# Issuing layer two's expert weights from SyncE and ScalarE in turn, with another order of work in the routing

## What is computed

```python
def _ec_moe(h, router, w_gate, w_up, w_down):
    B, n, _ = h.shape
    cap = CAPACITY_FACTOR * n // N_EXPERTS
    aff = jax.nn.softmax((h @ router).astype(jnp.float32), axis=-1)
    g, idx = lax.top_k(jnp.swapaxes(aff, 1, 2), cap)
    bidx = jnp.arange(B)[:, None, None]
    xs = h[bidx, idx]
    a = jnp.einsum('becd,edf->becf', xs, w_gate)
    u = jnp.einsum('becd,edf->becf', xs, w_up)
    y = jnp.einsum('becf,efd->becd', jax.nn.silu(a) * u, w_down) * g[..., None].astype(h.dtype)
    return jnp.zeros_like(h).at[bidx, idx].add(y)
```

## Time and profile before

| | us |
|---|---|
| median of 3 runs | 1863.23 |
| lowest and highest | 1861.32, 1863.63 |
| the profiled execution | 1864.48 |
| its span in the profile | 1862.6 |
| TensorE busy | 1764.9 (95%) |
| VectorE busy | 798.4 (43%) |
| ScalarE busy | 357.3 (19%) |
| GpSimd busy | 229.8 (12%) |

### The profile page before, as it was taken

The page is one execution under the profiler, slowest core; times in us unless marked ns, Lnnn a source line. Parts: engine busy times, 40 slices in busy tenths (PEclk is TensorE's granted clock), DMA queues, the critical chain, the costliest instruction groups (busy, mean ns, idle before and its releaser), DMA issues.

```text
span 1862.6 us, 30900 instructions
## 1 busy us (share of the span) xinstructions
PE 1764.9 (95%) x13222; PEld 900.6 (48%) x13222; DVE 798.4 (43%) x1624; ACT 357.3 (19%) x776; POOL 229.8 (12%) x313
## 2 busy tenths in 40 slices
PE   7999999999899999999999999999989999888896
PEld 4886567744344444444443886577433333222222
DVE  3994767678511111111112674776242333223232
ACT  3313455622100000000001313555210000000001
POOL 1000331011111112121111001410010000000000
PEclk9999999999899999999999999999999999999999
DMA  9644000086799999999997843001869999999996
GB/s 397 233 151 161 1 1 2 1 343 261 266 396 400 392 394 393 392 402 394 395 393 288 341 158 135 1 24 47 340 253 401 402 403 404 412 407 408 412 412 273
DMA packets 83137, 525.68 MB, mean 282 GB/s; under 512 B 11280, under 2 KB 13600, under 8 KB 24128
## 3 DMA queue, kind: packets, MB, share of 16 engines
q1 hardware_dynamic: 66672, 478.66, 63.9%
q0 software_dynamic: 14128, 44.84, 7.8%
q10 hardware_dynamic: 2208, 0.26, 0.1%
HBM read 506.94 MB, written 16.79 MB: 281 GB/s over the span
## 4 chain that ended last, share of the span: by engine, by line
PE 75%; DMA 15%; DVE 5%; ACT 3%; issue 1%; SPq 0%; POOL 0%; POOLq 0%; DVEq 0%; ACTq 0%
PE psum L1621 16%; PE psum L1615 9%; PE psum L1624 8%; DMA arena<-in_w_up 8%; PE psum L1495 7%; PE psum L1305 6%; PE psum L1263 6%; DMA ring<-in_w_up 6%; PE psum L1381 5%; PE psum L1426 3%; PE psum L1399 2%; PE psum L1355 2%; ACT arena L1086 2%; PE psum L1701 2%; PE psum L1339 2%
## 5 line engine op out<-in xcount | busy, mean ns | idle before, releaser
L1621 PE MATMUL psum<-ring,arena 128*32 128x512 f32 x1856 | 242.1, 593 | 0.0
L1615 PE MATMUL psum<-ring,arena 128*64 128x512 f32 x888 | 206.4, 600 | 19.4 <-DMA ring<-in_w_down 12.3
L1172 ACT ACTIVATE arena<-psum 128x768 f32<-128x768 f32 (+1 forms) x32 | 22.5, 704 | 894.5 <-PE psum L1624 463.3
L1615 PE MATMUL psum<-arena 128*64 128x512 f32 x648 | 151.3, 600 | 13.4 <-DMA arena<-in_w_up 7.4
L1495 PE MATMUL psum<-ring,arena 128*128 128x512 f32 x320 | 143.1, 598 | 0.8 <-DVE arena L2008 0.8
L1624 PE MATMUL psum<-ring,arena 128*32 128x256 f32 x1856 | 142.7, 379 | 0.0
L1086 ACT ACTIVATE arena<-psum,smx 128x768 f32<-128x768 f32 (+4 forms) x160 | 118.9, 748 | 96.4 <-DVE smx L1979 96.4
L1615 PEld LDWEIGHTS psum<-ring,arena 128*64 128x64 f32 x888 | 58.3, 136 | 151.1 <-issue 109.5
L1979 DVE TENSOR_REDUCE smx<-psum 128x1 f32<-128x768 f32 (+4 forms) x160 | 115.8, 765 | 30.9 <-PE psum L1339 23.9
L1624 PEld LDWEIGHTS psum<-ring,arena 128*32 128x32 f32 x1856 | 60.3, 110 | 138.8 <-issue 138.8
L1621 PE MATMUL psum<-arena 128*32 128x512 f32 x960 | 125.2, 593 | 0.0
(11 more groups left out here) (318 smaller groups left out, 2069.3 us busy)
## 6 DMA issues: line engine op xcount, KB each, us to landing
ring<-in_w_down SPq DMA_DIRECT2D x85, 1024.0 KB, 28.3
ring<-in_w_up SPq DMA_DIRECT2D x80, 1024.0 KB, 28.2
ring<-in_w_gate SPq DMA_DIRECT2D x78, 1024.0 KB, 28.0
arena<-in_w_gate SPq DMA_DIRECT2D x50, 1024.0 KB, 29.0
arena<-in_w_up SPq DMA_DIRECT2D x48, 1024.0 KB, 27.3
arena<-in_w_down SPq DMA_DIRECT2D x43, 1024.0 KB, 28.0
ring<-in_w_adat SPq DMA_DIRECT2D x32, 1024.0 KB, 6.3
ring<-in_w_in SPq DMA_DIRECT2D x18, 1024.0 KB, 19.9
```

Source lines behind the costliest of these rows:

```text
L1615: ins = mm(psum[64 * n:64 * n + 64, b * 512:(b + 1) * 512], lhs(k), w[:, n * 512:(n + 1) * 512], start=k == 0, stop=k == KD - 1)
L1621: ins = mm(psum[r0:r0 + 32, b * 512:(b + 1) * 512], lhs(k)[:, 32 * g:32 * g + 32], w[:, n * 512:(n + 1) * 512], start=k == 0, stop=k == KD ...
```

## The change

Four things change.

1. Expert weights of layer two: from m = 21 on SyncE issues the even quarters and ScalarE the odd ones (86 of them). SyncE skips those. ScalarE's program takes silu(0) first; then it goes through its quarters, waits for each one's place, issues it, and takes silu(e) as soon as the next place to wait for is one that comes free after the gate of e.
2. Layer one's quarters: 11 waits for the latent gather (`gl`); 12 to 14 wait only for w_out; 15 waits for expert 1's gather (`gat` at 32), the turned rows and the stores.
3. The routing's order. TensorE: in block 4's turn the logits of block 3 come after w_out's group 3 instead of 5, and the lists are turned there; the lists come across before the last group of block 5; the filler of three goes to one; the last logit parts come after the turn of the gathered latents. VectorE: affinities, lists, choosing, output and merging of the latents all lie in t = 4; the copy of turned rows goes ahead of the reciprocal in the last block; unit u = 2t + 1 of the ahead sums is made at t instead of t + 1, and GpSimd loads units 2t + 2 and 2t + 3 at t. ScalarE: the load of the exponential table goes behind the last copies, in both layers.
4. Attention: narrow steps alternate between half banks, so that the scores of a narrow step behind another wait for the exponentials of two steps before.

```diff
+    def narrow(st):
+        return st.kind == "W" and len(st.blocks) == NC
     def scores_at(st, x):
-        return 1024 * x
+        return 1024 * x + (512 * (st.i % 2) if narrow(st) else 0)
...
+    def by_scalar(l, m):
+        return l == DEPTH - 1 and m >= TURN[l] and m % 2 == 1
...
                     m = m0 + q
+                    if by_scalar(l, m):
+                        continue
...
+                    if l < DEPTH - 1 and m == RING + EARLY[l] - 1:
+                        sp.wait_ge(*LS[l]("gl", 16))
                     if m == RING + EARLY[l]:
                         sp.wait_ge(free, spent(where[("wout", l)]) + 4)
+                    if m == RING + EARLY[l] + UNDER_HT:
                         if l < DEPTH - 1:
-                            sp.wait_ge(*LS[l]("gl", 16))
+                            sp.wait_ge(*LS[l]("gat", 32))
                             sp.wait_ge(*LS[l]("ot", nq(l)))
...
-                    for u in (2 * t + 1, 2 * t + 2):
+                    for u in (2 * t + 2, 2 * t + 3):
...
-                if t == nq(l) - 1:
-                    act.activation(rootx[:], eps[:], ACT.Exp)
...
                 act.activation(lgpart[t % 2], bank(7, P, P * (t % 2)), ACT.Copy).then_inc(L["lc"], 1)
+                if t == nq(l) - 1:
+                    act.activation(rootx[:], eps[:], ACT.Exp)
...
+                silu(0, unit_no(l, 0, UP))
+                e = 1
+                for m, which, expert, q in long_units(l):
+                    if not by_scalar(l, m):
+                        continue
+                    place_free = spent(where[("exp", l)]) + m + 1 - TURN[l]
+                    if e < NE and place_free >= unit_no(l, e, GATE + 4 - UNITS_E):
+                        silu(e, unit_no(l, e, GATE + 4 - UNITS_E))
+                        e += 1
+                    dst, sem_of, _ = long_place(l, m)
+                    act.wait_ge(free, place_free)
+                    act.dma_start(dst.rearrange("p (k n) -> p k n", k=2), wv[which][expert, q]).then_inc(sem_of, 16)
+                while e < NE:
+                    silu(e, unit_no(l, e, GATE + 4 - UNITS_E))
+                    e += 1
...
+                if st.i >= 2 and apart(st):
+                    pe.wait_ge(*L("exp", 2 * st.i - 2))
+                elif st.i:
                     pe.wait_ge(*L("exp", 2 * st.i))
...
-                    slots_across(0)
-                    kept_busy(4, 3)
+                    kept_busy(4, 1)
...
-                if i == NX + 1:
-                    turn_lists(0)
+                sooner = i == NX and not last
                 if i < nq(l):
-                    mixed_rows(i, range(2, 4))
-                if i >= 1:
+                    mixed_rows(i, range(2, 3 if sooner else 4))
+                if i >= 1 and i != NX + 2:
                     logit_parts(i - 1)
+                if sooner:
+                    mixed_rows(i, range(3, 4))
+                    logits(i - 1)
                 if i < nq(l):
                     mixed_rows(i, range(4, 6))
+                if sooner:
+                    turn_lists(0)
...
                     ins.then_inc(L["xtl"], 1)
-                if i >= 1:
+                    logit_parts(i - 1)
+                if i >= 1 and not sooner:
                     logits(i - 1)
                 if i < nq(l):
-                    mixed_rows(i, range(6, 8))
+                    mixed_rows(i, range(6, 7))
+                if i == NX + 1:
+                    slots_across(0)
+                if i < nq(l):
+                    mixed_rows(i, range(7, 8))
...
                 if t == NX:
                     shifted(0)
+                    affinities(0)
+                    lists_in(0)
+                    for r in range(0, 2):
+                        best_eight(0, r)
...
-                if t == NX + 1:
-                    latents_merged()
                 tt(row_x(l, t), row_x(l, t), part, ALU.add).then_inc(L["x1"], 1)
                 if t == NX:
-                    affinities(0)
+                    best_eight(0, 2)
...
                 if not last and t < NX:
-                    if t >= 1:
-                        ahead_sums(2 * t - 1)
                     ahead_sums(2 * t)
+                    if t < NX - 1:
+                        ahead_sums(2 * t + 1)
                 if t == NX:
-                    lists_in(0)
-                    for r in range(CAPX // 8):
+                    for r in range(3, CAPX // 8):
                         best_eight(0, r)
                     slots_out(0)
+                    latents_merged()
```

More of the change, by code:

```diff
@@ L182, in build_program @@
     EARLY = [0, 4]
+    UNDER_HT = 3
+    assert UNDER_HT * SLOT == 8 * T
     assert DEPTH == 2
@@ L652, in expert_loads, with long_units @@
         return ([(0, 0)] if e == 0 else []) + [(1, e)] + ([(0, e + 1)] if e < NE - 1 else []) + [(2, e)]
+    def by_scalar(l, m):
+        return l == DEPTH - 1 and m >= TURN[l] and m % 2 == 1
+    def long_units(l):
+        m = 0
+        for e in range(NE):
+            for which, expert in expert_loads(l, e):
+                for q in range(4):
+                    yield m, which, expert, q
+                    m += 1
     def unit_no(l, e, m):
@@ L1172, in silu @@
                 act.activation(sg[l][:, 0:n_col], psum[:, 1024:1024 + n_col], ACT.Silu).then_inc(L["silu"], 1)
[L1174 to L1177, removed]
+            if l < DEPTH - 1:
+                for e, _ in body_experts(act):
+                    silu(e, unit_no(l, e, UP) if isinstance(e, int) and e == 0
+                         else unit_no(l, e, GATE + 4 - UNITS_E))
+                silu(NE - 1, unit_no(l, NE - 1, GATE + 4 - UNITS_E))
+            else:
+                silu(0, unit_no(l, 0, UP))
+                e = 1
+                wv = [w[l] for w in (w_gate, w_up, w_down)]
+                for m, which, expert, q in long_units(l):
[11 more added lines that the diff above has]
+                    e += 1
             act.activation(rootx[:], eps[:], ACT.Sqrt)
@@ L1327, in _, with apart @@
             steps = ATT[l]
+            def apart(st):
+                return narrow(st) and narrow(steps[st.i - 1])
             def scores(st):
-                if st.i:
+                if st.i >= 2 and apart(st):
+                    pe.wait_ge(*L("exp", 2 * st.i - 2))
+                elif st.i:
                     pe.wait_ge(*L("exp", 2 * st.i))
@@ L2092, in shifted @@
                 dve.wait_ge(*L("lg", b1))
+                dve.wait_ge(*L("orc", b1))
                 for t in range(b0, b1):
@@ L2182, in _ @@
                 dlink(dve, tt(part, bank(2 * (t % 2), D), g1row[s], ALU.mult))
-                if t == NX + 1:
-                    latents_merged()
                 tt(row_x(l, t), row_x(l, t), part, ALU.add).then_inc(L["x1"], 1)
                 if t == NX:
-                    affinities(0)
-                dve.wait_ge(*L("ort", t + 1))
-                dve.reciprocal(stat[:, 2, t:t + 1], stat[:, 1, t:t + 1]).then_inc(L["orc"], 1)
+                    best_eight(0, 2)
+                if t < nq(l) - 1:
+                    dve.wait_ge(*L("ort", t + 1))
+                    dve.reciprocal(stat[:, 2, t:t + 1], stat[:, 1, t:t + 1]).then_inc(L["orc"], 1)
                 dve.wait_ge(*L("ot", t + 1))
```

## The result

The changed kernel takes 1872.15 us (median), the kernel before, in runs beside it, 1863.63: a ratio of 1.0045, interval 1.0034 to 1.0056. It is slower by 8.5 us, and outside the range of 1857.5 to 1869. In the profiled executions the span grew by 7.7 us, from 1862.6 to 1870.3.

| start of | before | after | shift | change since the row above | forecast |
|---|---|---|---|---|---|
| w_out, layer one | 376.80 | 375.29 | -1.5 | -1.5 | -0.5 |
| turn of expert 1's rows | 508.71 | 496.89 | -11.8 | -10.3 | -6.9 + 0.6 |
| layer two's projections | 1023.79 | 1020.80 | -3.0 | +8.8 | +0.9 |
| w_out, layer two | 1293.66 | 1291.27 | -2.4 | +0.6 | 0 |
| first product of layer two's experts | 1386.28 | 1383.56 | -2.7 | -0.3 | -0.9 |

What follows compares the result with a forecast made beforehand. Layer one was taken as led by TensorE with DMA also full, layer two as set by weight landings. Terms -6.0 + 0.6 - 0.5 - 0.9 + 0 + 2.3 + 4.9 = +0.4 gave 1863.6 us, range 1857.5 to 1869.

Steps and rivals of the forecast that it cites:

- The end of layer two: Last weight landings of layer two: two queues with equal turns keep SyncE's head start, quarter 187 lands later, +4.9 us.
- The start: Layer two's first expert quarters: ScalarE issues quarter 21 only behind silu(0), the DMA engines lose time, +2.3 us (0.5 to 3).
- The issue: ScalarE's issues in layer two's experts: 2.1 us each in front of its silus, absorbed before UP's quarters land, nothing.
- The rate: Weights' transfer rate in layer two on two queues: packet for packet in turn and no faster, 0 (-5.6 to +2).
- Routing in layer one: Between layer one's attention and first joint product: earlier scaling and faster gathers, less the stream's cost, -6.0 us (-2.5 to -7.5).
- What that costs: Layer one's held quarters: TensorE's lead of 7.3 us becomes 7.3 - 6.9 - 1.2 = -0.8, so it waits some 0.9 us.
- the sign that the forecast had named for its fall: End of layer one: the forecast falls if that layer ends less than 4 us sooner.
- the attention: Narrow steps of layer one's attention may start their scores one step sooner, -0.5 us (-1.8 to 0).
- the ahead units: Unit 3 of the ahead sums, loaded and summed one block sooner, holds up VectorE's add of t=1, +0.6 us (0 to 3).
- Layer two's routing: The exponential table's load moves behind the last copy of turned rows, off the last logits' path, -0.9 us (-1.5 to 0).
- Rival 2: Layer one: gathers stay slow alone, held quarters make the stream 4.8 us late, routing gives 2.5; 1867.1 us, chance 0.16.
- Rivals 1, 3 and 4: 1: odd quarters keep up, 1859.1 us, 0.17; 3: two queues faster, 1858.0, 0.09; 4: second queue changes nothing, 1856.4, 0.08.

## Why the prediction was wrong

**The end of layer two** was right: +4.9 forecast, +5.0 measured. The head start of SyncE's queue is made in the first microseconds and kept for 450, as the equal packet counts of the earlier trace rows said; the run with the last 24 quarters on SyncE gave back 4.9, and the one with ScalarE first showed that the head start comes from the issue behind silu(0).

**The start** was right: +2.3 forecast, 2.4 measured. ScalarE's first quarter went out 0.6 us sooner than forecast, with silu(0) issued and not yet done.

**The issue** was right in what it came to, nothing, and not in its size: ScalarE's issues took 3.3 and 3.6 us in the rows above, not 2.1, and SyncE's 0.33. Five of the fifteen later silus came behind such an issue, and TensorE waited for none of them.

**The rate** was wrong: 0 was taken, with +2 as the upper end; it cost 2.9 us in 410. The step put "packet for packet in turn and no faster: 0" between two windows of the earlier trace rows with no gather in either. The windows were right, the rate away from gathers is 421 GB/s on one queue and on two, but the stage has a gather per expert, and with these beside it the second queue is not free: 405 GB/s instead of 408. The row that would have told was that of the whole stage in the earlier trace rows: 409 GB/s against the 423 of a stretch without a gather. That gap of 14 GB/s was there to be explained; without gathers it is gone, and with the second queue it is larger. The Trainium skill (DMA: Bandwidth & Descriptors, "Issuing engines are not separate DMA queues") says that issuing from several engines saves the issue time alone. The pair without gathers agrees, 421 and 421; with gathers 3 us were lost.

**Routing in layer one** failed at the step "What that costs", and there at the sum 7.3 - 6.9 - 1.2 = -0.8. The mechanism was the right one, but its main size and one of its ends were off. Counted from w_out's start, the gain was 10.3 us and not 6.9. The scaling came 4.4 us sooner, as forecast, but none of it was lost on the way: the latents were turned 4.9 us sooner and not 3.75. GATE0 followed this by 2.9 us and not by 3.45 + 0.4, and so began 5.4 us sooner and not 3.3. From there to the turn of expert 1's rows 4.9 us fell away and not 3.56: the waits shrank by 2.4 only, but TensorE's work took 2.5 us less at a granted clock of 1.00 instead of 0.89. The clock stood in no term of the sum. The stream of weights then ended 0.3 us later from w_out on, and not 1.2. Against a TensorE that is 10.3 us sooner the lead of 7.3 was overdrawn by 3.3: the sum reads 7.3 - 10.3 - 0.3 = -3.3 instead of -0.8. What I left out is the end: when TensorE is that far ahead of the stream, the residual rows' loads run beside the last quarter and the weights behind it, and VectorE waits for these too. TensorE ended layer one's products 6.5 us sooner and began the next layer 3.0 us sooner. Of 11.8 us, 8.8 went back, where the forecast had 0.9. So the sign that the forecast had named for its fall, layer one ending less than 4 us sooner, came. The thirteen traces show what a better step would have said: the next layer's first expert product follows the landing of layer one's last quarter by 378.4 to 381.0 us, so here the new order was worth what it did to the stream and little more.

**The rest**: the attention gave 1.5 us with all that precedes it (0.5 forecast; runs differ by that much there, so it is not shown), the ahead units cost nothing to be seen, where +0.6 was forecast. Layer two's routing gained 0.3 instead of 0.9: its lists and its gather were some 1.4 us sooner within the stage, and the filler at a lower clock gave 1.1 of it back.

**Of the rivals**, none came. Rival 2 had the right place, layer one's stream and the held quarters, but the wrong cause: the gathers were as fast as hoped, and the loss came anyway. Two of its figures were wrong besides: the context gather had five quarters beside it before and not six, and with the gathers' 2.46 and 1.97 us added to 500.7 its landing is 505.1 and not 504.3, which makes its time 1868.0 us and not 1867.1. Rivals 1, 3 and 4 fell with the order of the landings and with the rate.

In sum: -6.0 + 0.6 for layer one's routing became -1.5 (3.9 us more), 0 for the rate became 3, and smaller terms (-1.0 up to w_out, +0.6 in layer two's projections and attention, +0.6 in its routing) make up the rest of the way from +0.4 to +7.7 in the span.

## What to carry to other kernels

Where two resources are both nearly full, as TensorE and the DMA engines were in layer one, a stage that starts sooner need not end sooner (11.8 us became 3.0): find the last landing and ask what the change does to that. An ordered stream split over two queues kept the head start that one of them got at the first issue to the end, and the last consumer paid 4.9 us for it, so the engine that issues the first transfer should have nothing in front of it. The second queue added no rate (421 GB/s on one and on two), and the gathers beside the stream became dearer (8.1 us and 9.7), so rate is to be read from a stage with all that runs in it.

## What the runs showed of the hardware

In layer one's routing gathers of 4 KB rows took 2.8 to 3.0 us (32 rows), 3.7 to 4.0 (64) and 4.3 to 4.7 (96) with little or nothing of the weights beside them, and 6.4 to 9.5 beside their stream. Two weights' queues shared the DMA engines packet for packet, 8075 to 7969, and a skew between them of little over one quarter of 1 MB lasted through 85 quarters each. A stretch without gathers moved 421 GB/s, on one queue and on two. In the routing before the change TensorE's granted clock was 0.50 over 3.45 us and 0.89 over the 25.91 behind them; in the changed kernel it was 1.00 in both stretches.
